# A fused two-block transformer kernel on one core: the transposed activations of the two up projections moved to 64 bytes below a multiple of 256, and a small rope table fetched later

## The reference, cut to what matters

```python
def conv_ffn(h, w_up, w_conv, b_conv, w_down):        # block 1, D_FF = 5632
    z = h @ w_up
...
    gate, val = jnp.split(z, 2, axis=-1)
    return (jax.nn.gelu(gate) * val) @ w_down
...
        k_rope = apply_rope(k_r, cos, sin)            # block 2
...
        m = rms_norm_2(h, norm_ffn[l])                # block 2, D_FF_2 = 5632
        h = h + (jax.nn.silu(m @ w_ffn_gate[l]) * (m @ w_ffn_up[l])) @ w_ffn_down[l]
```

## Time and profile before

| what | value |
|---|---|
| median of three runs | 3224.5 us |
| profiled execution | 3222.92 us |
| its span in the trace | 3221.1 us |
| TensorE busy | 3063.3 us, 95% of the span |
| VectorE, ScalarE, GpSimd busy | 1804.5, 1271.6, 322.9 us |
| granted TensorE clock, mean | 0.97 of full |

### The profile page before, as it was taken

The page is one execution under the profiler, slowest core; times in us unless marked ns, Lnnn a source line. Parts: engine busy times, 40 slices in busy tenths (PEclk is TensorE's granted clock), DMA queues, the critical chain, the costliest instruction groups (busy, mean ns, idle before and its releaser), DMA issues.

```text
span 3221.1 us, 43193 instructions
## 1 busy us (share of the span) xinstructions
PE 3063.3 (95%) x18045; PEld 2649.4 (82%) x18045; DVE 1804.5 (56%) x1704; ACT 1271.6 (39%) x1155; POOL 322.9 (10%) x460
## 2 busy tenths in 40 slices
PE   8899999996999999999698999989998999999998
PEld 3588777875999999888586888867777999999886
DVE  1476777786676766444545446654544444444444
ACT  0134554333444444343333333434433444444333
POOL 1000000001000000000106826610000000000000
PEclk9899999998999999999798999989998999999999
DMA  9776777893666655655345652226643455445554
GB/s 359 267 286 261 285 274 289 308 370 132 234 229 219 234 196 184 223 208 208 132 167 184 213 179 75 86 79 249 216 167 130 182 182 182 182 182 196 209 209 168
DMA packets 110498, 671.55 MB, mean 208 GB/s; under 512 B 23520, under 2 KB 25696, under 8 KB 33312
## 3 DMA queue, kind: packets, MB, share of 16 engines
q1 hardware_dynamic: 101584, 626.96, 53.4%
q0 software_dynamic: 8800, 42.97, 3.5%
HBM read 652.48 MB, written 17.40 MB: 208 GB/s over the span
## 4 chain that ended last, share of the span: by engine, by line
PE 90%; DVE 5%; DMA 2%; ACT 1%; issue 1%; SPq 0%; POOL 0%; DVEq 0%; POOLq 0%; ACTq 0%
PE acc L1798 27%; PE acc L1800 26%; PE acc L1799 26%; PE ms L1868 3%; PE tp L1843 2%; DVE w_lo L1129 1%; DMA w_raw<-w_stream 1%; DVE mod_sum L1204 1%; PE ms L2233 1%; PE acc L2262 0%; PE acc L2272 0%; DVE y L1170 0%; DMA ada<-ada_stream 0%; DMA w_raw<-ada_stream 0%; PE ms L2232 0%
## 5 line engine op out<-in xcount | busy, mean ns | idle before, releaser
L1129 DVE TENSOR_TENSOR w_lo<-w_raw,w_hi 128x2048 fp32r<-128x2048 f32 x484 | 1111.1, 2303 | 869.7 <-ACT w_hi L754 850.4
L754 ACT ACTIVATE w_hi<-w_raw 128x2048 fp32r<-128x2048 f32 x484 | 922.7, 1913 | 1084.9 <-DMA w_raw<-w_stream 1083.1
L1798 PE MATMUL acc<-h2T_hi,w_lo 128*128 128x256 f32 x2816 | 798.2, 283 | 3.4 <-DVE h2T_lo L1143 3.4
L1800 PE MATMUL acc<-h2T_hi,w_hi 128*128 128x256 f32 x2816 | 797.6, 283 | 0.0
L1799 PE MATMUL acc<-h2T_lo,w_hi 128*128 128x256 f32 x2816 | 797.5, 283 | 0.0
L1798 PEld LDWEIGHTS acc<-h2T_hi,w_lo 128*128 128x128 f32 x2816 | 541.4, 192 | 4.0 <-issue 4.0
L1799 PEld LDWEIGHTS acc<-h2T_lo,w_hi 128*128 128x128 f32 x2816 | 541.3, 192 | 0.0
L1800 PEld LDWEIGHTS acc<-h2T_hi,w_hi 128*128 128x128 f32 x2816 | 541.3, 192 | 0.0
L1798 PE MATMUL acc<-w_hi,hid_lo 128*128 128x512 f32 x704 | 275.0, 391 | 4.5 <-DVE w_lo L1129 4.5
L1799 PE MATMUL acc<-w_lo,hid_hi 128*128 128x512 f32 x704 | 274.6, 390 | 0.0
L1800 PE MATMUL acc<-w_hi,hid_hi 128*128 128x512 f32 x704 | 274.6, 390 | 0.0
(11 more groups left out here) (503 smaller groups left out, 3970.5 us busy)
## 6 DMA issues: line engine op xcount, KB each, us to landing
w_raw<-w_stream SPq DMA_DIRECT2D x484, 1024.0 KB, 4.8
ada<-ada_stream SPq DMA_DIRECT2D x64, 1024.0 KB, 6.9
w_raw<-ada_stream SPq DMA_DIRECT2D x32, 1024.0 KB, 6.1
g_dram<-gates_out SPq DMA_DIRECT2D x12, 512.0 KB, 7.1
gates_in<-g_dram POOLq DMA_DIRECT2D x12, 512.0 KB, 5.7
bias_rows<-b_in POOLq DMA_DIRECT2D x18, 256.0 KB, 6.1
x_res<-x POOLq DMA_DIRECT2D x2, 2048.0 KB, 13.1
g_dram<-gate_stage SPq DMA_DIRECT2D x8, 512.0 KB, 6.1
```

The source lines that it names most:

```text
L754: sc.activation(whi[:, s % 4], raw[:, s % 4], ACT.Copy).then_inc(hi_made, 1)
L1129: v.tensor_tensor(wlo[:, s % 4], raw[:, s % 4], whi[:, s % 4].bitcast(F32), ALU.subtract).then_inc(lo_made, 1)
L1798: mm(o, sl, mh, start=start, stop=False, skip_group_check=share)
L1800: return mm(o, sh, mh, start=False, stop=stop, skip_group_check=share)
```

## The change

The rope table leaves the small tensors, and is fetched by GpSimd in the second block, into a place in the big region that is free from then on (17 KB above U); it gets a semaphore of its own, for which VectorE waits ahead of the key rotation. The space of 768 bytes is taken out of the layout: `U` goes from 87.5 to 86.75, so every tensor of the big region (but those placed by `X0`, which is 64 - U above it) moves down by 768 bytes, three times 256. `h2T_hi` and `h2T_lo` are placed a further 64 bytes lower, so that each of their pieces starts 192 bytes past a multiple of 256. Nothing else is placed so, and no arithmetic changes.

```diff
-        rope = small("rope_tab", [P, 2, 3, 32])
...
-        U = 87.5
-        assert pos[0] <= U, pos
+        B64 = 64 / K
+        U = 86.75
+        assert pos[0] <= U - 2 * B64, pos
...
-        h2T = [u("h2T_hi", [P, KD, S], 0, F32R), u("h2T_lo", [P, KD, S], 16, F32R)]
+        h2T = [u("h2T_hi", [P, KD, S], -B64, F32R), u("h2T_lo", [P, KD, S], 16 - B64, F32R)]
...
+        rope = u("rope_tab", [P, 2, 3, 32], 17)
...
-            fetch("small", rope[:], a["rope"])
             fetch("small", ssmd[:], a["ssm_d"])
...
             for t in range(TT):
                 rsqrt_mean(D, [(P, t, t + 1)])
+            fetch("rope", rope[:], a["rope"])
 
             pool.dma_start(a["x_dram"], x[:]).then_inc(sem("x_saved"), 16)
...
-            act.wait_ge(sem("ld_small"), 64)
+            act.wait_ge(sem("ld_small"), 48)
...
-            dve.wait_ge(sem("ld_small"), 64)
+            dve.wait_ge(sem("ld_small"), 48)
...
+            dve.wait_ge(sem("ld_rope"), 16)
             dve.wait_ge(sem("kr"), 1)
```

## The result

The changed kernel takes 3180.3 us (median of 4 executions, 3179.2 to 3182.0), the kernel before on the same chip 3223.8 us (4 executions). The ratio is 0.9867, with a 95% interval of 0.9850 to 0.9883: 43.5 us faster. The sign was right and the time lies inside the forecast range; the forecast gain of 15.6 us was little more than a third of the measured one.

A forecast was written before the change was run, and what follows sets the result against it. TensorE, busy 95% of the span, was taken as the bound. Terms of -15.6 us and zeros on 3222.9 us gave 3207.3, plus 1.6 for the median: 3209 us, range 3165 to 3245.

The forecast's parts named there:

- The reading of the gap: Up projections: 120 ns a multiply is 107 streaming plus 13 gap; 110 us might depend on where operands lie.
- Part (1): Up projections: moving h2T by 64 bytes changes each of 8448 multiplies by -1.85 ns, -15.6 us.
- Evenly, in both blocks alike: Up projections: starts in block 1 should come every 118 ns, evenly, and the same in both blocks.
- wrong in size: Up projections: sign that the gain was misjudged, h2T rows near 276 ns, the 16-token pace plus 163.
- the pace plus 163: Up projections: a multiply's duration is its start-to-start pace plus 163 ns, so mean durations show changes of pace.
- The bound of the 16-token rows: Up projections: at best the 113 ns of kvT pieces with 16 tokens, -59 us, 3165 us; chance 0.12.
- The independent read ports: TensorE: a documented rule of separate ports for moving operand and weight load; start address makes no difference, zero gain.
- Part (2): All other tensors of the big region: shifting them 768 bytes, three times 256, costs or gains zero.
- Part (3): VectorE and ScalarE write h2T 64 bytes lower, 16 instructions each, no change of size: zero.
- Part (4): Rope load in the second block: lands by about 1573, 20 us to spare; zero, bounds 0 to 1 us.
- The slower rival: Up projections: displaced stream meets the weight load worse, 2.3 ns a multiply, 19 us, 3244 us; chance 0.27.
- the far end: Up projections: +7 ns a multiply from nT rows with 512 columns, +59 us, kept outside the range; chance 0.1.

The follow-up runs named there:

- the narrow loads: Changed kernel with h2T back at a multiple of 256, up projections loading only 16 of 128 weight columns and writing 16 partitions: 3190.7 and 3163.1 us.
- the displaced weights: Changed kernel with h2T back at a multiple of 256 and the weights, x and small tensors 64 bytes up instead: 3191.7 us, ratio 0.9895.
- the four waits: Changed kernel with TensorE waiting for its own modulation product before the next chunk, four times in block 1: 3189.7 us, ratio 0.9910.

## Why the prediction was right in sign and wrong in size

**What bounds the kernel.** Right. The gain is TensorE's alone, and nothing else became late: in the 40 us windows it is busy for 40.00 us at either pace. The reading of the gap, 13 ns over 107 of streaming and partly the meeting of stream and weight load, fits the narrow loads, which take away up to half of it (though they narrow the output too). That all of it "might depend on where operands lie" was too much: no kernel went below a gap of 6.7 ns.

**Part (1), the price of the move, is the step that failed.** The mechanism was right, the term of -1.85 ns was mis-sized; measured from starts, it is (2688 x 2.2 + 5760 x 6.7) / 8448 = 5.3 ns, and 4.7 by the mean durations. I took "the middle of their -2.8 and -0.9 ns", from rows in which the distance between the operands changes from piece to piece, and noted that no row shows an operand that stays at one place. The runs put a price of its own on each place. From the times in the table, the pace falls by -0.4, 1.4, 5.1, 2.2, 1.1, 0.1, 2.2 and 3.3 ns at the eight places from 0 to 224 (the difference to the kernel before over 8448 multiplies). The change has one of these places, and the best one. Over the four multiples of 64 that the rows run through (0, 64, 128, 192) the mean is 2.0 ns, near what I forecast, but that is no derivation: my 1.85 is the middle of two unlike numbers, and by their starts the `nT` multiplies follow every 126.1 ns, 119.4 without their 16 more columns, a gain of only 0.6 ns. That the forecast came near the mean of the places is luck, as far as the runs show.

Nor would splitting the `nT` rows by piece have helped. By the starts in the trace before, the three multiplies on the piece at 192 bytes take 125, 127 and 129 ns to the next start; less 6.7 for the 16 more columns this is 120.3, no gain, while the pieces at 0 come out best, at 118.1. So pieces among neighbours at other places don't show the pace that their place gives when thousands follow each other alike. I read this as the state that one multiply leaves to the next, which the kept paces of the stretches suggest too; no run tests it.

**"Evenly, in both blocks alike" and 281 ns, 2378 us together** were wrong: 279 ns, 2353.9 us, two paces, and block 2 gained 26 us to block 1's 16. The sign for "wrong in size", `h2T` rows near 276, held where the pace was 113.3 (median 277 in the window 2600 to 2640) and not where it was 117.8 (282 in 1120 to 1160). That the duration is the pace plus 163 held too. The bound of the 16-token rows, 113 ns, was the right floor, and I gave it 0.12 since those loads read an eighth of the bytes. The narrow kernel shows that this doubt was partly sound, since at distance 0 it reaches that pace in some stretches; but with whole loads, the place gives it too.

**The independent read ports** of the Trainium skill ("SBUF — State Buffer", section "Who interferes with whom") would have made the change worth nothing. At 160 bytes the trace agrees with that, 120.0 ns as at 0; at 32, 64, 192 and 224 bytes in every stretch, at 96 and 128 in most (118.7 down to 113.3 ns), and at 512 columns (233.3 for 226.7), it does not.

**Part (2), zero for 768 bytes:** right for the time, 3225.2 us with everything but the 64 bytes, and for `hid`. The sign that went with it, `nT` rows within 1 ns of the earlier trace rows, failed for two groups of three (396 to 401 and 398 to 396), without a cost: their sum stayed, and the repetition of the same layout reads 396 again. **Part (3):** right, nothing in VectorE's or ScalarE's busy time. **Part (4), the rope load:** right, issue at 1549.88, landed after 2.2 us, needed 24 us later; the work between the up projections lasts 1159 us where it lasted 1158.

**The slower rival** (a bad fixed distance) did not occur at 256 columns at any of eight places. At 512 columns it is real, 6.6 ns for `hid`, near the 6 to 8 ns of the `nT` rows from which I took the far end. The width is why that end did not apply here: the same distance in the same direction gains at 256 columns.

**What stays open.** Which state of TensorE the two paces are, why the distance matters at all, and what makes one stretch fall into the one or the other. Shown are only that a pace is taken within a few multiplies of an interruption or of the clock's rise, that a directly preceding one-column product gave the slower in 24 of 24, and that it then stays for as long as the stretch lasts, up to some 4200 multiplies.

## What to carry to other kernels

Before costing a placement, read TensorE's pace from start to start and set it against what the columns need; of a constant remainder over it a placement may give back a part (here up to half). Then try the one placement: where the distance between the operands varies from multiply to multiply, neither the mean of the rows nor a single piece among them prices a distance that is held for thousands of multiplies. The sign at one width says nothing on another: 64 bytes gave 2 to 7 ns at 256 columns and cost 2 to 7 at 512.

A kernel whose multiplies can fall into more than one steady pace has a spread of its own: the displaced weights took 3179 to 3203 us and the four waits 3173 to 3198, where a single stretch explains 2 to 19 us. The spread alone doesn't tell, though: the 8 executions of the changed kernel lie within 10 us, 3176 to 3186, and the kernel before, with one pace, spreads by 14 us in 19 executions (3213.9 to 3227.4, the shorter ones mostly at a slightly higher mean clock, 0.971 to 0.973 for 0.967 to 0.969). Compare windows of single stretches, not only whole times.

## What the runs showed of the hardware

- A run of equal multiplies of 256 columns at full clock keeps one of a few paces, to within 0.1 ns in the mean of 192, for up to some 4200 multiplies. In the profiled executions these were 113.3 or 117.8 ns with the moving operand 64 bytes below the stationary one's place in 256 bytes, three paces (117.3, 118.7, 120.0) at 96 bytes, two at 128 (118.7, 120.0), and one at 0, 32, 160, 192 and 224. Single steps scatter around it by place: every step is 119 or 120 ns at 0, they run from 115 to 126 at 160 and from 113 to 120 at 224.
- The distance counts in steps finer than 64 bytes: 32 bytes gave 118.3 ns, 96 gave others than 64 and 128.
- A fall to half the clock and back can change the pace: 113 ns before it and 117.8 behind it in block 2 with the displaced weights.
- The mean duration of the weight loads changed, though their size and the weights' place did not: 188 to 189 ns in the changed kernel, as in

```profile
L1800 PEld LDWEIGHTS acc<-h2T_hi,w_lo 128*128 128x128 f32 x2816 | 530.3, 188 | 4.0 <-issue 4.0
```

  against 192 before. Within one kernel it moves with the pace (187.8 ns in the stretches at 113.3, 189.3 in those at 117.8), but it is no measure of the pace: at 160 bytes the loads take 188.3 ns at the same 120.0 ns as before. So a load's duration in the trace is not the load's own cost alone; what the rest is, no run shows.
